# SiLU of a convolution branch: from the Silu table after all tiles to exp, reciprocal and product tile by tile

## The chip, the cores and the metric

The kernel is one program on one core of a Trainium2 chip. The metric is device time in microseconds of the whole program; the time before is the median of three executions. The profile is of one further execution, whose span is counted from its first to its last instruction.

Engines are named as in the profile: PE is TensorE, ACT ScalarE, DVE VectorE, POOL GpSimd, SP the engine that issues nearly all loads. Each takes its instructions strictly in the order in which the program lists them, and semaphores alone tie the engines together.

## The reference, cut to what matters

Two blocks of two layers each run over 512 tokens of 1024 channels in float32. The change lies in the last layer's mixer. It projects the input, runs a forgetting attention with 8 heads of 64 over half of the channels and a convolution branch over the other half, and projects both back:

```
def conformer_conv(p_d, dw_w, dw_b, cn_g, cn_b):
    h = p_d[..., :D_D] * jax.nn.sigmoid(p_d[..., D_D:])
    h = causal_dwconv(h, dw_w) + dw_b              # 31 taps
    h = layer_norm(h, cn_g, cn_b)                  # over 512 channels
    return jax.nn.silu(h)                          # h / (1 + exp(-h))

y_c = forgetting_attention(q, k, v, log_f)
y_d = conformer_conv(p[..., 3 * D_C + H_C:], dw_w, dw_b, cn_g, cn_b)
return jnp.concatenate([y_c, y_d], axis=-1) @ w_out
```

## The kernel before

Every matrix product is made of three PE passes over high and low halves of its operands, so each weight tile that SP loads into `raw` is first split: ACT copies the rounded high half (`split_w`, L464), POOL subtracts it for the low half (L817). Each such tile is called a unit. PE waits for a unit's low half before its first product with it.

The last mixer interleaves everything by hand in a loop over `s` from 0 to 16, written once for each engine. Here it is called step `s`. `p, qb = divmod(s, 4)` is the pair of heads and the block of 128 queries. In step `s` of `p < 3`

- PE makes the logits of both heads (L1580, banks 4 and 5, n = 128 (qb + 1) columns), then projection products for the next pair (L975 to L977); in between it transposes the probabilities of step `s - 1` (`p_transposes`, L1064, banks 6 and 7). At `qb == 0` it also transposes the values (`v_transposes`, L1080, bank 6), at `qb == 1` it multiplies the probabilities of the previous pair with its values (`attend`, L1086, bank 6). From step 12 on the projection products are those of the mixer's output (`odd_out`, L1025 to L1027).
- DVE adds biases and finds the row maximum (`forget_logits`, L2068 and L2071), inverts the row sums (`inverse_sums`, L1769), and copies each finished projection tile out of its bank (L1641: value, Q, K). At `qb == 0` PE does not begin the new logits until DVE has copied the K tile of the step before (`tile_free`).
- ACT takes the exponentials (`exp_row`, L556), scales them (`scale_row`, L565), and copies the transposed probabilities of step `s - 1` out of banks 6 and 7 (`keep_p`, L572).

A bank is written again only once its reader has signalled: 4 and 5 by `lg_free`, 6 and 7 by `tr_free` or `va_free`.

The convolution branch rides along. In steps 5 to 7 its four channel tiles are transposed to tokens through bank 3 (`rows_of`), DVE takes mean and variance of each token, in step 8 ACT scales and shifts the token rows `fz` (L785). In steps 9 and 10 PE transposes them back, one channel tile of 128 x 512 at a time, into bank 3 (`cols_of`, L1533), and ACT copies each into `fC` (`keep_cols`, L724). In step 11, behind its `keep_p`, ACT applies Silu with the channel's gain and bias to all four (L792). Silu stands in another activation table than the exponential, so the profile has an ACT_TABLE_LOAD ahead of the four and another behind them, before the exponentials of step 12 (L556). In steps 12 and 13 ACT and POOL split `fC` into `XH` and `XL` (L476, L831).

ACT splits one unit in each of the steps 1, 5, 9, 12 and 14.

Of the kernel before, what the change touches and what calls it, by code (L numbers as in the profile page):

```python
# [26 lines left out]
F32 = mybir.dt.float32  # L27
F32R = mybir.dt.float32r
ALU = mybir.AluOpType
ACT = mybir.ActivationFunctionType  # L30

P = 128
S = 512
# [132 lines left out]
def build(nc, x, xT, par, con, rcon, gb, w, out):  # L166
    ctx = ExitStack()
    with ctx:
        def sb(name, shape, dt=F32, stack=ctx):
            return stack.enter_context(nc.sbuf_tensor(name, shape, dt))  # L170
# [146 lines left out]
        cwH = sb("cwH", [P, TAPS], F32R, ph)  # L317
        cwL = sb("cwL", [P, TAPS], F32, ph)
        partmax = sb("partmax", [P, 4], F32, ph)
        fBD1 = sb("fBD1", [P, S], F32, ph)  # L320
        fsig = sqt
        fB = [sq, fB1]
# [64 lines left out]
        cn_ready = sem("cn_ready")  # L387
        rows_scaled = sem("rows_scaled")
        to_cols = sem("to_cols")
        cols_kept = sem("cols_kept")  # L390
        swished = sem("swished")
        rows_out = sem("rows_out")
        gate_in = [sem(f"gate_in{i}") for i in range(2)]
        gate_ready = sem("gate_ready")
# [58 lines left out]
        def _(act):  # L453
# [264 lines left out]
                act.wait_ge(to_rows, t + 1)  # L718
                act.copy(fz[t][:, 0:S], bank[3][:]).then_inc(rows_kept, 1)

            def keep_cols(c):

                act.wait_ge(to_cols, c + 1)
                act.copy(fC[:, c, :], bank[3][:]).then_inc(cols_kept, 1)  # L724

            def gate_biases(p):

# [29 lines left out]
            for s in range(17):  # L757
                p, qb = divmod(s, 4)
                if s < 16:
                    n, c = (qb + 1) * P, 2 * (s % 2)  # L760
                    for m in range(2):
                        exp_row(fL[s % 2][m][:, 0:n], negmax[:, c + m:c + m + 1], rowsum[:, c + m:c + m + 1])
                    if qb == 0 and p < 3:
                        gate_biases(p + 1)
                    sums_inverted()
                    for m in range(2):
                        scale_row(fL[s % 2][m][:, 0:n], rinv[:, c + m:c + m + 1])
                    if qb == 0:
                        vax.add()
                if qb == 1 and p:  # L770
                    odd_high(p - 1)
                if s in (6, 7):
                    keep_rows((1, 3)[s - 6])
                if s in (9, 10):
                    keep_cols((0, 2)[s - 9])
                for m in range(2) if s else ():
                    keep_p(fPT[m], 6 + m, (s - 1) % 4)
                if s == 5:
                    keep_conv(3, conv_done, 3)
                if s in (5, 6):  # L780
                    keep_rows((0, 2)[s - 5])
                if s == 8:
                    act.wait_ge(cn_ready, 1)
                    for t in range(NB):
                        act.activation(fz[t][:, 0:S], fz[t][:, 0:S], ACT.Identity, bias=st[:, 3 * NB + t:3 * NB + t + 1],  # L785
                                       scale=root[:, t:t + 1]).then_inc(rows_scaled, 1)
                if s in (9, 10):
                    keep_cols((1, 3)[s - 9])
                if s == 11:
                    act.wait_ge(cols_kept, 4)  # L790
                    for c in range(4):
                        act.activation(fC[:, c, :], fC[:, c, :], ACT.Silu, bias=pcol("cn_b", c), scale=pcol("cn_g", c)).then_inc(swished, 1)  # L792
                if qb == 1 and p < 3 or s in (12, 14):
                    split_w()
                if s == 12:
                    act.wait_ge(tile_free, tiles.at())
                if s in (12, 13):
                    for k in ((4, 5), (6, 7))[s - 12]:
                        split_at(XH[:, k, :], fC[:, k - 4, :], swished, k - 3)
                if p < 3 and qb == 3:  # L800
                    tiles.add(3)
# [7 lines left out]
        def _(pool):  # L809
# [119 lines left out]
            split_w()  # L929
            inverse_root()  # L930
            diagonal_biases(3)
            split_w(2)
            for k in (4, 5, 6, 7):
                split_x(XL[:, k, :], fC[:, k - 4, :], XH[:, k, :])
            split_w()
# [7 lines left out]
        def _(pe):  # L943
# [584 lines left out]
            def cols_of(c):  # L1528

                pe.wait_ge(rows_scaled, NB)  # L1530
                claim(3)
                for t in range(NB):
                    ins = pe.transpose(bank[3][:, t * P:(t + 1) * P], fz[t][:, c * P:(c + 1) * P], ident)  # L1533
                ins.then_inc(to_cols, 1)
                freed[3] = (cols_kept, c + 1)

            def odd_attend(p):

# [31 lines left out]
            for s in range(16):  # L1570
                p, qb = divmod(s, 4)
                i, n = p % 2, (qb + 1) * P
                if qb == 0:
                    pe.wait_ge(tile_free, tiles.at())
                    off = begin_unit()
                claim(4)
                claim(5)
                for m in range(2):
                    half = slice(64 * m, 64 * m + 64)
                    logit_end(pe.matmul(bank[4 + m][:, 0:n], fQ[i][half, qb * P:n], fK[i][half, 0:n], start=True, stop=True), 4 + m)  # L1580
                if qb == 0:
                    v_transposes(6, fVT, tiles.at())
                if qb == 1 and p:
                    odd_attend(p - 1)
                if p < 3:
                    pair_steps(off, ODD_SLOTS[2 * qb])
                    if qb == 3:
                        pair_steps(off, ODD_SLOTS[7])
                elif qb:
                    odd_out((1, 5, 7)[qb - 1])  # L1590
                if s in (6, 7):
                    rows_of((1, 3)[s - 6])
                if s in (9, 10):
                    cols_of((0, 2)[s - 9])
                for m in range(2) if s else ():
                    p_transposes(6 + m, fL[(s - 1) % 2][m], (s - 1) % 4 + 1)
                if p < 3 and qb < 3:
                    pair_steps(off, ODD_SLOTS[2 * qb + 1])
                if s == 14:
                    off = begin_unit()  # L1600
                if p == 3 and qb < 3:
                    odd_out((0, 4, 6)[qb])
                if s in (5, 6):
                    rows_of((0, 2)[s - 5])
                if s in (9, 10):
                    cols_of((1, 3)[s - 9])
            los.add(4)
            for m in range(2):
                p_transposes(6 + m, fL[1][m], NB)
# [7 lines left out]
        def _(dve):  # L1617
# [416 lines left out]
                        ins.then_inc(conv_done, 1)  # L2034

            glu(0)
            dve.wait_ge(cw_hi, 1)
            dve.tensor_tensor(cwL[:], parm[:, PCOL["dw_w"]:PCOL["dw_w"] + 4 * TAPS:4], cwH[:].bitcast(F32), ALU.subtract).then_inc(cw_lo, 1)
            take(lambda: dve.tensor_scalar(lfz[:], bank[2][0:8, :], parm[0:8, PCOL["f_b"]:PCOL["f_b"] + 1], None, ALU.add))
# [44 lines left out]
            for s in range(17):  # L2084
# [24 lines left out]
                if s == 8:  # L2109
                    row_stats(3)  # L2110
                    dve.tensor_scalar(st[:, 2 * NB:3 * NB], moment[:, :, 1], LN_EPS, None, ALU.add).then_inc(var_ready, 1)
                    roots.add()
                    dve.wait_ge(root_ready, roots.at())
                    dve.scalar_tensor_tensor(st[:, 3 * NB:4 * NB], moment[:, :, 0], -1.0, root[:], ALU.mult, ALU.mult).then_inc(cn_ready, 1)
            assert not taps_left
            los.add(5)
            out_projection()
# [121 lines left out]
```

## Time and profile before

| | |
|---|---|
| median of 3 executions | 2341.62 us (2339.07 to 2342.72) |
| the profiled execution, own time | 2339.27 us |
| its span | 2337.5 us |
| PE busy | 2282.1 us, 98% |
| POOL, ACT, DVE busy | 1037.9, 706.2, 703.8 us |
| granted TensorE clock, mean | 0.994 of full |
| chain that ended last: PE | 88% |
| chain that ended last: DVE, ACT | 7%, 3% |
| ACT_TABLE_LOAD, all | 12, 1283 ns each |

The profiled execution's own time is 1.8 us longer than its span: that much lies around it. The two loads that the change speaks of are two of the twelve. A busy share says little for one stage; the stage in question lies between 1870 and 1915 us of the span.

### The profile page before, as it was taken

To read this page: it belongs to the slowest core of one execution; us is meant where nothing else is said; L and a number is where in the kernel's file an instruction comes from. 1 tells how busy PE (TensorE), PEld (TensorE's weight loads), DVE (VectorE), ACT (ScalarE), POOL (GpSimd) and SP (SyncE) were. 2 spreads that over 40 slices of the span, in tenths; PEclk is the share of its full clock that TensorE was granted. 3 is DMA by queue.
4 is the path that set the end of the run, shared out by engine and by line. 5 is a ranking of instruction groups with operands and counts; after the bars stand their busy time and mean duration, and the time that the engine had idled before them with its cause. 6 is when DMAs were issued, how large, how long until landed. Compare 5 with 4: busy or idle time off the path is not lost.

```text
span 2337.5 us, 24617 instructions
## 1 busy us (share of the span) xinstructions
PE 2282.1 (98%) x10287; PEld 1835.8 (79%) x10287; DVE 703.8 (30%) x1351; ACT 706.2 (30%) x1002; POOL 1037.9 (44%) x359
## 2 busy tenths in 40 slices
PE   8999999999999999999999999999999999999998
PEld 6667888888776778888878888888877667888887
DVE  7535000004476450000057320000158635000003
ACT  2443231222344332212222232222244563221220
POOL 3224454454323255545545645445442334554543
PEclk9999999999999999999999999999999999999999
DMA  4213222322221133222223332322222113332221
GB/s 170 72 74 125 104 96 93 106 72 72 90 73 73 54 108 99 99 91 98 99 73 112 108 109 93 106 90 88 79 90 87 51 67 106 111 108 91 93 88 54
DMA packets 33534, 214.72 MB, mean 92 GB/s; under 512 B 3720, under 2 KB 4872, under 8 KB 10000
## 3 DMA queue, kind: packets, MB, share of 16 engines
q1 hardware_dynamic: 32256, 211.03, 26.0%
q10 hardware_dynamic: 1168, 2.11, 0.3%
q8 instruction: 82, 1.34, 0.2%
q14 instruction: 28, 0.23, 0.0%
HBM read 211.02 MB, written 2.11 MB: 91 GB/s over the span
## 4 chain that ended last, share of the span: by engine, by line
PE 88%; DVE 7%; ACT 3%; issue 1%; POOL 0%; DMA 0%; SPq 0%; DVEq 0%; ACTq 0%
PE bank L975 16%; PE bank L977 16%; PE bank L976 16%; PE bank L1025 9%; PE bank L1027 9%; PE bank L1026 9%; DVE bank L2030 2%; PE bank L1086 2%; PE bank L1161 2%; PE bank L1162 2%; PE bank L1166 2%; PE bank L1204 1%; PE bank L1459 1%; PE bank L1006 1%; PE bank L1064 1%
## 5 line engine op out<-in xcount | busy, mean ns | idle before, releaser
L817 POOL TENSOR_TENSOR wlo<-raw,whi 128x2048 fp32r<-128x2048 f32 (+5 forms) x184 | 843.6, 4586 | 603.1 <-ACT whi L464 594.8
L975 PE MATMUL bank<-XH,whi 128*128 128x512 f32 x1752 | 692.1, 395 | 10.8 <-POOL wlo L873 6.1
L977 PE MATMUL bank<-XH,wlo 128*128 128x512 f32 x1752 | 684.6, 391 | 0.0
L976 PE MATMUL bank<-XL,whi 128*128 128x512 f32 x1752 | 683.8, 390 | 0.0
L464 ACT CAST whi<-raw 128x2048 fp32r<-128x2048 f32 (+5 forms) x184 | 349.6, 1901 | 416.5 <-PE bank L1025 304.5
L975 PEld LDWEIGHTS bank<-XH,whi 128*128 128x128 f32 x1752 | 330.4, 189 | 93.5 <-issue 16.3
L977 PEld LDWEIGHTS bank<-XH,wlo 128*128 128x128 f32 x1752 | 330.0, 188 | 69.8
L976 PEld LDWEIGHTS bank<-XL,whi 128*128 128x128 f32 x1752 | 330.5, 189 | 66.5
L1729 DVE TENSOR_TENSOR hf<-sil,bank 128x512 f32<-128x512 f32 x80 | 55.0, 687 | 814.4 <-PE bank L977 814.4
L1025 PE MATMUL bank<-whi,HH 128*128 128x512 f32 x704 | 274.4, 390 | 0.0
L1027 PE MATMUL bank<-wlo,HH 128*128 128x512 f32 x704 | 274.0, 389 | 0.0
L1026 PE MATMUL bank<-whi,HL 128*128 128x512 f32 x704 | 273.9, 389 | 0.0
L831 POOL TENSOR_TENSOR HL<-hf,HH 128x512 fp32r<-128x512 f32 x80 | 103.5, 1294 | 376.2 <-ACT HH L512 376.2
L512 ACT CAST HH<-hf 128x512 fp32r<-128x512 f32 x80 | 49.6, 621 | 453.0 <-DVE hf L1729 453.0
L1025 PEld LDWEIGHTS bank<-whi,HH 128*128 128x128 f32 x704 | 132.1, 188 | 27.4
L1026 PEld LDWEIGHTS bank<-whi,HL 128*128 128x128 f32 x704 | 132.2, 188 | 27.3
L1027 PEld LDWEIGHTS bank<-wlo,HH 128*128 128x128 f32 x704 | 132.1, 188 | 27.4
L1669 DVE SCALAR_TENSOR_TENSOR X<-X,bank 128x512 f32<-128x512 f32 x64 | 43.9, 687 | 278.1 <-PE bank L1027 277.6
L508 ACT ACTIVATE sil<-bank 128x512 f32<-128x512 f32 x80 | 47.8, 598 | 186.2 <-PE bank L977 186.2
L847 POOL TENSOR_TENSOR troot<-tvar,neg_half 128x1 f32<-128x1 f32 x32 | 25.6, 799 | 129.6 <-DVE tvar L1695 129.6
L489 ACT CAST XH<-bank 128x512 fp32r<-128x512 f32 x56 | 30.7, 589 | 155.4 <-PE bank L1204 155.0
L2030 DVE SCALAR_TENSOR_TENSOR bank<-fz,parm,bank 128x512 f32<-128x512 f32 x90 | 68.0, 755 | 3.0
(270 smaller groups left out, 2231.6 us busy)
## 6 DMA issues: line engine op xcount, KB each, us to landing
raw<-w_ffn_gu SPq DMA_DIRECT2D x88, 1024.0 KB, 4.8
raw<-w_ffn_dn SPq DMA_DIRECT2D x40, 1024.0 KB, 4.8
GB<-gb SPq DMA_DIRECT2D x8, 1024.0 KB, 6.8
raw<-w_diff_in SPq DMA_DIRECT2D x6, 1280.0 KB, 6.2
raw<-w_ev_in SPq DMA_DIRECT2D x6, 1024.0 KB, 4.9
raw<-w_od_in SPq DMA_DIRECT2D x4, 1536.0 KB, 6.4
raw<-w_mla_pair SPq DMA_DIRECT2D x4, 1088.0 KB, 5.6
raw<-w_mla_o SPq DMA_DIRECT2D x4, 1024.0 KB, 6.1
```

The lines of the kernel that those rows point to most:

```text
L464: act.copy(whi[:, off:off + size], raw[:, off:off + size]).then_inc(hi_ready, 1)
L512: act.copy(HH[:, j, :], hf[i][:]).then_inc(act_hi, 1)
L817: pool.tensor_tensor(wlo[:, off:off + size], raw[:, off:off + size], whi[:, off:off + size].bitcast(F32), ALU.subtract).then_inc(lo_ready, 1)
L831: pool.tensor_tensor(dst, src, hi.bitcast(F32), ALU.subtract).then_inc(act_lo, 1)
L975: release(pe.matmul(out, whi[:, off:off + P], xh, start=start, stop=False))
L976: pe.matmul(out, whi[:, off:off + P], xl, start=False, stop=False)
L977: return pe.matmul(out, wlo[:, off:off + P], xh, start=False, stop=stop)
L1025: release(pe.matmul(bank[b][:], xh[:, rows], whi[:, off:off + HALF], start=start, stop=False))
L1026: pe.matmul(bank[b][:], xl[:, rows], whi[:, off:off + HALF], start=False, stop=False)
L1027: ins = pe.matmul(bank[b][:], xh[:, rows], wlo[:, off:off + HALF], start=False, stop=stop)
L1729: take(lambda: dve.tensor_tensor(hf[i][:], sil[i][:], bank[2 * i + 1][:], ALU.mult), 2)
L2030: ins = dve.scalar_tensor_tensor(acc, fz[i][:, k:k + S], wk, acc, ALU.mult, ALU.add)
```

## The change: SiLU from the exponential table

`y / (1 + exp(-y))` is worked out with `y = g z + b`, where `z` is the normalised channel tile in bank 3 and `g`, `b` are the channel's gain and bias.

- Once, early in the mixer, DVE makes `negcn`, the negated gains and biases.
- For each channel tile ACT takes `ey = exp(-g z - b)` straight from bank 3. There is one buffer `ey`, so the next exponential waits until the tile before has been finished (`swished`).
- DVE makes `fC = g z + b` from bank 3 (which frees the bank, `norm_kept`), then `ey + 1`, then the reciprocal of it (`inverted`).
- POOL multiplies `fC` by `ey` (`swished`).
- The four tiles are handled in three steps: tile 0 in step 9, 1 and 2 in step 10, 3 in step 11. PE's transposes move with them.
- ACT's weight split of step 9 stands at the end of step 8.

```
-            def keep_cols(c):
+            def exp_cols(c):
                 act.wait_ge(to_cols, c + 1)
-                act.copy(fC[:, c, :], bank[3][:]).then_inc(cols_kept, 1)
+                if c:
+                    act.wait_ge(swished, c)
+                act.activation(ey[:], bank[3][:], ACT.Exp, bias=negcn[:, 4 + c:5 + c], scale=negcn[:, c:c + 1]).then_inc(exp_kept, 1)
...
-                if s in (9, 10):
-                    keep_cols((0, 2)[s - 9])
+                if s in (9, 10, 11):
+                    exp_cols((0, 1, 3)[s - 9])
                 for m in range(2) if s else ():
                     keep_p(fPT[m], 6 + m, (s - 1) % 4)
...
-                if s in (9, 10):
-                    keep_cols((1, 3)[s - 9])
-                if s == 11:
-                    act.wait_ge(cols_kept, 4)
-                    for c in range(4):
-                        act.activation(fC[:, c, :], fC[:, c, :], ACT.Silu, bias=pcol("cn_b", c), scale=pcol("cn_g", c)).then_inc(swished, 1)
-                if qb == 1 and p < 3 or s in (12, 14):
+                if s == 10:
+                    exp_cols(2)
+                if s in (1, 5, 8, 12, 14):
                     split_w()
...
-            split_w(2)
+            def swish(c):
+                pool.wait_ge(inverted, c + 1)
+                pool.tensor_tensor(fC[:, c, :], fC[:, c, :], ey[:], ALU.mult).then_inc(swished, 1)
+            split_w()
+            for c in range(4):
+                swish(c)
+            split_w()
...
-                freed[3] = (cols_kept, c + 1)
+                freed[3] = (norm_kept, c + 1)
...
-                if s in (9, 10):
-                    cols_of((0, 2)[s - 9])
+                if s in (9, 10, 11):
+                    cols_of((0, 1, 3)[s - 9])
...
-                if s in (9, 10):
-                    cols_of((1, 3)[s - 9])
+                if s == 10:
+                    cols_of(2)
...
+            dve.tensor_scalar(negcn[:], parm[:, PCOL["cn_g"]:PCOL["cn_g"] + 8], -1.0, None, ALU.mult)
...
+                for c in {9: (0,), 10: (1, 2), 11: (3,)}.get(s, ()):
+                    dve.wait_ge(exp_kept, c + 1)
+                    dve.tensor_scalar(fC[:, c, :], bank[3][:], pcol("cn_g", c), pcol("cn_b", c), ALU.mult, ALU.add).then_inc(norm_kept, 1)
+                    link(dve.tensor_scalar(ey[:], ey[:], 1.0, None, ALU.add))
+                    dve.reciprocal(ey[:], ey[:]).then_inc(inverted, 1)
```

ACT before, from the copy of the last channel tile (end of step 10) to the first table load behind the four Silu (`fL10`, `fL11` are the logits of step 11, `rinv` its inverted sums):

```order
L724 COPY fC<-bank3 128x512 [waits to_cols]
L556 ACTIVATE fL10,rowsum<-fL10,negmax 128x512 [waits lg_free]
L556 ACTIVATE fL11,rowsum<-fL11,negmax 128x512 [waits lg_free]
L565 ACTIVATE fL10<-fL10,rinv 128x512 [waits rec_ready]
L565 ACTIVATE fL11<-fL11,rinv 128x512
L572 COPY fPT0<-bank6 128x3x128 [waits tr_done]
L572 COPY fPT1<-bank7 128x3x128 [waits tr_done]
L792 ACT_TABLE_LOAD
L792 ACTIVATE fC<-fC,parm 128x512 [waits cols_kept]
L792 ACTIVATE fC<-fC,parm 128x512 x3
L556 ACT_TABLE_LOAD
```

ACT now, the same stretch from the exponential of tile 1 in step 10 to the copies of transposed probabilities in step 11:

```order
L730 ACTIVATE ey<-bank3,negcn 128x512 [waits swished,to_cols]
L576 COPY fPT0<-bank6 128x2x128 [waits tr_done]
L576 COPY fPT1<-bank7 128x2x128 [waits tr_done]
L730 ACTIVATE ey<-bank3,negcn 128x512 [waits swished,to_cols]
L560 ACTIVATE fL10,rowsum<-fL10,negmax 128x512 [waits lg_free]
L560 ACTIVATE fL11,rowsum<-fL11,negmax 128x512 [waits lg_free]
L569 ACTIVATE fL10<-fL10,rinv 128x512 [waits rec_ready]
L569 ACTIVATE fL11<-fL11,rinv 128x512
L730 ACTIVATE ey<-bank3,negcn 128x512 [waits swished,to_cols]
L576 COPY fPT0<-bank6 128x3x128 [waits tr_done]
L576 COPY fPT1<-bank7 128x3x128 [waits tr_done]
```

The two table loads and the four Silu are gone from between the copies and step 12's exponentials; an exponential of a channel tile that waits for `swished` now stands ahead of step 11's row exponentials, and another ahead of its copies.

DVE before, from the inverted row sums of step 10 through the logits of step 11 (ISA is the combined add and minimum of `forget_logits`):

```order
L1769 RECIPROCAL rinv<-rowsum 128x2 [waits exp_done]
L1641 COPY fQ1<-bank1 128x512 [waits tile_done]
L2068 ISA fL10,partmax<-bank4,sq0 128x384 [waits lg_done]
L2068 ISA partmax 128x1
L2071 ISA fL10,negmax<-bank4,shift,partmax 128x128 [waits step]
L2071 ISA negmax 128x1
L2068 ISA fL11,partmax<-bank5,sq1 128x384 [waits lg_done]
L2068 ISA partmax 128x1
L2071 ISA fL11,negmax<-bank5,fBD0,partmax 128x128 [waits step]
L2071 ISA negmax 128x1
L1769 RECIPROCAL rinv<-rowsum 128x2 [waits exp_done]
L1641 COPY fK1<-bank2 128x512 [waits tile_done]
```

DVE now, the same stretch up to the first logits of step 11:

```order
L1780 RECIPROCAL rinv<-rowsum 128x2 [waits exp_done]
L1652 COPY fQ1<-bank1 128x512 [waits tile_done]
L2129 TENSOR_SCALAR fC<-bank3,parm 128x512 [waits exp_kept]
L2130 TENSOR_SCALAR ey<-ey 128x512
L2131 RECIPROCAL ey<-ey 128x512 [waits step]
L2129 TENSOR_SCALAR fC<-bank3,parm 128x512 [waits exp_kept]
L2130 TENSOR_SCALAR ey<-ey 128x512
L2131 RECIPROCAL ey<-ey 128x512 [waits step]
L2080 ISA fL10,partmax<-bank4,sq0 128x384 [waits lg_done]
L2080 ISA partmax 128x1
L2083 ISA fL10,negmax<-bank4,shift,partmax 128x128 [waits step]
L2083 ISA negmax 128x1
```

Six instructions for tiles 1 and 2 have come between the Q tile's copy and the logits of step 11, and the first of each three waits for ACT's exponential.

## Rows read from the trace of the kernel before

**Rows 1.** Page, part 1: busy us, share of span and instructions by engine.
```profile
PE 2282.1 (98%) x10287; PEld 1835.8 (79%) x10287; DVE 703.8 (30%) x1351; ACT 706.2 (30%) x1002; POOL 1037.9 (44%) x359
```

**Rows 2.** ACT in order of time: start us, duration us, engine, line, operation.
```profile
1896.30 1.34 ACT L565 ACTIVATE fL<-fL,rinv 128x512 f32<-128x512 f32 x2 [0.23 <-DVE rinv L1769]
1898.05 0.86 ACT L572 COPY fPT<-bank 128x384 f32<-128x384 f32 x2 [0.41 <-PE bank L1064]
1898.93 1.28 ACT L792 ACT_TABLE_LOAD   x1
1900.22 2.94 ACT L792 ACTIVATE fC<-fC,parm 128x512 f32<-128x512 f32 x4
1903.18 1.28 ACT L556 ACT_TABLE_LOAD   x1
1906.18 1.05 ACT L572 COPY fPT<-bank 128x512 f32<-128x512 f32 x2
```

**Rows 3.** PE in order of time, idle time ahead of it in brackets.
```profile
1876.44 3.93 PE L1086 MATMUL bank<-fPT,fV 128*64 128x512 f32 x16
1883.16 0.60 PE L1533 MATMUL bank<-cons,fz 128*128 128x128 f32 x4
...
1900.42 1.06 PE L1064 MATMUL bank<-cons,fL 128*128 128x128 f32 x8 [0.88 <-DVE fV L2092]
1907.28 5.60 PE L1086 MATMUL bank<-fPT,fV 128*64 128x512 f32 x16 [2.41 <-ACT fPT L572]
```

**Rows 4.** One stretch: busy us by engine, TensorE clock, DMA share, GB/s.
```profile
1907.30:1911.20 3.90, 3.90 (x10) 1.59 (x11) 0.11 (x1) 3.76 (x7) 2.09 (x1) 0.58 0.00 0
```

**Rows 5.** DVE in order of time, steps 10 to 12.
```profile
1886.67 0.42 DVE L2068 CUSTOM_DVE_ANT_0 fL<-bank,sq 128x256 f32<-128x256 f32 x1 [3.98 <-PE bank L1580]
1893.39 0.56 DVE L2068 CUSTOM_DVE_ANT_0 fL<-bank,sq 128x384 f32<-128x384 f32 x1 [3.07 <-PE bank L1580]
1897.72 0.69 DVE L1641 COPY fK<-bank 128x512 f32<-128x512 f32 x1 [1.45 <-PE bank L977]
1899.10 0.29 DVE L2071 CUSTOM_DVE_ANT_0 fL<-bank,sqt 128x128 f32<-128x128 f32 x1 [0.69 <-PE bank L1580]
1899.58 0.69 DVE L2092 COPY fV<-bank 128x512 f32<-128x512 f32 x1
```

**Rows 6.** ACT in order of time, steps 8 to 10.
```profile
1875.07 2.93 ACT L785 ACTIVATE fz<-fz,st,root 128x512 f32<-128x512 f32 x4
1886.32 1.91 ACT L464 CAST whi<-raw 128x2048 fp32r<-128x2048 f32 x1
1889.66 1.12 ACT L565 ACTIVATE fL<-fL,rinv 128x384 f32<-128x384 f32 x2 [0.23 <-DVE rinv L1769]
```

**Rows 7.** By source line: count, ns min/median/max, first and last start.
```profile
L2003 DVE TENSOR_SCALAR EY<-bank,parm x4: 742/744/751, 1282.8 to 1284.8; 128x512 f32<-128x512 f32 x4
L1998 DVE TENSOR_SCALAR EY<-ez,parm x4: 486/722/1007, 1251.5 to 1280.7; 128x512 f32<-128x512 f32 x4
L785 ACT ACTIVATE fz<-fz,st,root x4: 806/808/827, 1875.1 to 1877.2; 128x512 f32<-128x512 f32 x4
L831 POOL TENSOR_TENSOR XL<-fC,XH x4: 1276/1296/1305, 1913.6 to 1918.3; 128x512 fp32r<-128x512 f32 x4
```

**Rows 8.** DVE by source line: two reciprocals, two tensor products.
```profile
L1769 DVE RECIPROCAL rinv<-rowsum x32: 154/166/167, 68.7 to 1929.6; 128x2 f32<-128x2 f32 x32
L1911 DVE RECIPROCAL rinv<-rowsum x32: 162/164/167, 613.7 to 799.1; 128x1 f32<-128x1 f32 x32
L1990 DVE TENSOR_TENSOR EP<-EP,eu x4: 176/176/178, 1227.7 to 1249.9; 128x16 f32<-128x16 f32 x4
L2005 DVE TENSOR_TENSOR EY<-bank,EY x4: 692/692/692, 1289.4 to 1305.8; 128x512 f32<-128x512 f32 x4
```

**Rows 9.** A DVE source line; a POOL weight subtraction in order of time.
```profile
L1985 DVE TENSOR_TENSOR eu<-eu x10: 691/1178/4336, 1226.0 to 1247.3; 128x512 f32<-128x512 f32 x10
1888.31 4.60 POOL L817 TENSOR_TENSOR wlo<-raw,whi 128x2048 fp32r<-128x2048 f32 x1 [9.55 <-ACT whi L464]
```

More of the change, by code:

```diff
@@ L319, in build @@
         partmax = sb("partmax", [P, 4], F32, ph)
+        negcn = sb("negcn", [P, 8], F32, ph)
+        ey = sb("ey", [P, S], F32, ph)
         fBD1 = sb("fBD1", [P, S], F32, ph)
@@ L389, in build @@
         to_cols = sem("to_cols")
-        cols_kept = sem("cols_kept")
         swished = sem("swished")
+        exp_kept = sem("exp_kept")
+        inverted = sem("inverted")
+        norm_kept = sem("norm_kept")
         rows_out = sem("rows_out")
```

## The prediction

> **What bounds the kernel now.** First the page: TensorE is busy for 2282.1 of 2337.5 us and every other engine for less than half [rows 1]. So a change to ACT, DVE or POOL is worth only what PE waits for it, and I read the stage around the change in order of time. PE and ACT first, from the end of step 11. ACT scales the probabilities of step 11 at 1896.30, copies the transposed ones of step 10 until 1898.91, then has the first table load, four Silu and the second load, 1.28 + 2.94 + 1.28 = 5.5 us in which it can serve nobody; its copy of step 11's transposed probabilities ends at 1907.23 [rows 2]. The product of probabilities and values in step 13 needs that copy and sits idle for 2.41 us, until 1907.28 [rows 3]. It then takes 5.60 us where its twin in step 9 took 3.93: the granted clock is 0.58 of full over that stretch [rows 3, 4], a mixture of the two levels, 1.2 and 2.4 GHz, and what came before was PE's idle time. So the Silu block is on the path with 2.41 us of wait and, by the difference of the twins, 1.67 us of slow clock. Earlier PE waits 0.88 us for DVE's copy of the values, which ends at 1900.27 [rows 3, 5]. These 4.96 us are all that this stage can give.
>
> **What goes.** The two loads and four Silu, and four copies out of bank 3. With them the 2.41 us would go, if nothing else were late.
>
> **What comes, per channel tile.** ACT's exponential with two operands per partition: 0.81 us (L785, the same form). DVE: the affine from PSUM 0.74 (L2003); `ey + 1` in SBUF 0.49 (L1998's minimum, a form that reached 1.01 beside POOL) [rows 7]. The reciprocal of 512 columns is not in the trace. Two ends: 0.49 if it went as the fastest SBUF form. For the other end, two columns cost 166 ns and one 164 by the medians, so 2 ns for one more, and 510 of those on 166 make 1.19. The tensor products go from 176 ns at 16 columns to 692 at 512, 1.04 ns a column [rows 8]; at that slope the reciprocal is 0.166 + 0.53 = 0.70, the value I take, since it lies on a row's slope between the ends. DVE per tile: 0.74 + 0.49 + 0.70 = 1.93. POOL's product: 1.30, as L831 [rows 7]. One tile from ACT's start to POOL's end is 0.81 + 1.93 + 1.30 = 4.04 us, and with one buffer `ey` the next may not begin earlier.
>
> **Tile 0, step 9: hidden, with nothing to spare.** ACT's scaling of `fz` ends at 1878.0, the split moved behind it takes 1.91 and ends at 1879.9 [rows 6]. That delays step 9's exponentials by about 1.9 us, but PE is in the product of step 9 until 1880.4 and ACT reaches the cast behind it by 1882.0. The transposes of tile 0 leave PE at 1883.76 [rows 3], exponential until 1884.6, DVE until 1886.5. DVE's logits of step 10 start at 1886.67 before [rows 5] and some 0.4 earlier now, since a group of transposes has gone from ahead of them: late by about nothing. ACT no longer has the 1.91 us split in front of step 10's exponentials, so they are slightly earlier.
>
> **Tiles 1 and 2, step 10: on the path.** DVE's logits of step 10 at 1886.6 lead to ACT's scaling about 2.5 us later, at 1889.1 (step 11 with 512 columns takes 2.91, below), and the scaling takes 1.12 [rows 6]; exponential of tile 1 from 1890.2 to 1891.0; DVE until 1892.95; POOL until 1894.25. ACT stands in front of tile 2's exponential, which ends at 1895.1, and DVE is through at 1897.1. Only then, in DVE's order, come step 11's logits, which were begun at 1893.39: 3.7 us late. Queued behind ACT's wait are step 11's row exponentials, behind DVE's the logits, the inverted sums and the K tile. From the first logit to the scaling it was 1896.30 - 1893.39 = 2.91 [rows 2, 5], so the scaling starts at 1900.0 and the K copy, behind the inverted sums, ends at 1900.7 instead of 1898.41 [rows 5]. PE may not begin step 12 before it: 2.3 us late.
>
> **Tile 3, step 11.** ACT scales until 1901.35, takes tile 3 until 1902.15, copies step 10's transposed probabilities (0.86) until 1903.0 [rows 2]; PE's transposes of values wait for that in bank 6. DVE finishes tile 3 at 1904.1, takes 0.48 for step 12's logits (1899.10 to 1899.58) and 0.69 for the values [rows 5]: 1905.3. PE's transposes of step 11 follow at 1905.35 instead of 1900.42, 4.9 us late.
>
> **Where it ends.** From those transposes to the product in step 13 it was 1907.28 - 1900.42 = 6.86 us, of which 2.41 were the wait [rows 3]. ACT, free of the block, is done with its copy at about 1907.5, so only the 4.45 us of PE work count: the product begins at 1909.8 instead of 1907.28, **2.5 us later**. Three waits (K copy, ACT's bank 6, value copy) of about 2 us each have taken the place of two. They leave PE mostly idle between 1898.5 and 1905.3, more than before, so I expect the slow clock again, a little earlier and at about the same 1.67 us; that term cancels. If it did not come the sum would be +0.8, if it came twice +4.2.
>
> The rest costs nothing that I can see: the first constant `negcn` is one DVE instruction of 0.2 us early in the mixer, ahead of a correction that ACT needs only several small operations later; the high half of the first output unit is ready earlier, its low half by 1884.5,, so the load that waits for its place is issued earlier. Behind step 13 the program is the same and everything moves along.
>
> Sum: the profiled execution's own 2339.27 + 2.5 = 2341.8. The median of the runs lies 2.35 above that execution, so 2344.1 on the scale of the median.
>
> **The unknown costs.** The reciprocal counts three times on the path (tiles 1, 2, 3), and above 0.70 four times, since tile 0 had nothing to spare. At 0.49: 3 x 0.21 = 0.6 less, +1.9. At 1.19: 4 x 0.49 = 2.0 more, +4.5.
>
> **Rival 1, slower: the reciprocal is iterated for every column.** Place: DVE, all four tiles. At eight passes of a row's 1.04 ns per column [rows 8] it is 512 x 8 x 1.04 + 0.16 = 4.42 us, 3.72 more than in my sum, four times over: 14.9, so +17.4 and 2359. It decides from about 1.25 us on, where the sum reaches 0.2%. Against it: a second column would then add 8 ns, and adds 2, and no reciprocal of the 64 took over 167 ns. For it: two columns are few, and a start-up that hides the first passes could look like this. 15%. The Trainium skill speaks for it ("VectorE: DVE Perf Modes", Walkthrough: the 8-slice pipeline in each mode, First, the fixed hardware budget): it says that reciprocal runs by iterative divide with a repeat count of 8 on the same pipe. Whether that count is per column it does not say, and the trace's 2 ns disagree with that reading.
>
> **Rival 2, faster: the waits vanish.** If DVE were through with tile 2 before PE's logits of step 11 (1893.39) [rows 5], nothing would be late, and the 2.41 + 0.88 + 1.67 of today would go: 2336.7. It needs 3.7 us less than two serial tiles cost by the rows; only hand-offs and instructions at half their rows would do. 6%.
>
> **Rival 3, slower: DVE held by POOL.** `ey + 1` is of the form that took 0.49 to 1.01, and a DVE line with two SBUF inputs went from 0.69 to 4.34 us beside POOL [rows 7, 9]. If POOL's subtraction for the unit (4.60 us) [rows 9] began a us later than the 1879.9 worked out, it would still run when tile 0 needs the port at 1885.3, and hold it by up to 4.6 us: +2.5 to +7.1, 2348.7 at most. For: only 0.9 us separate them. Against: nothing that ACT waits for ahead of that split is late. 9%. The Trainium skill has the rule ("SBUF — State Buffer", two separate sides): a Vector operation in a two-port mode and a GpSimd operation lock each other out for a whole instruction. The stretched rows agree.
>
> That the change doesn't do what it says, with table loads elsewhere, I give 1%: between the exponentials of steps 0 and 16 no other table is asked for, and the copies and affines needed none before.
>
> **How the numbers follow.** My case 69%: 2344.1, its own range 2341 to 2347 from the bounds of reciprocal and clock. About 0.2% (4.7 us) is what a measurement of this kernel can tell from no change. Rivals 1 (15%) and 3 (9%, two thirds of it beyond) and 5% of mine above it make slower 0.27; rival 2 makes faster 0.06; the rest is same, 0.67. The range from 2339.5 to 2350 holds mine and rival 3 and leaves out rival 1 and most of 2.
>
> **What would show it.** Two ACT_TABLE_LOAD fewer (10). No ACT idle time ended by PE but two waits of ACT for POOL's product of about 2.5 us ahead of the exponentials of tiles 2 and 3 or of DVE behind them. PE idle three times between 1898 and 1906, put down to DVE's K copy, ACT's copy out of bank 6 and DVE's value copy. No wait of the product in step 13 for ACT. The reciprocal at 0.70 us: above 1.2 my sum fails, at over 4 rival 1 stands. A tile 2 exponential before 1892 would refute the serial chain.

## The result: 2355.1 us, 0.58% slower

After: 2355.11 us, median of 4 runs (2353.68 to 2356.17). Before, on the same chip: 2340.53 us (2339.07 to 2342.72, 4 runs). The ratio is 1.0058, 95% interval 1.0046 to 1.0070, or +13.6 us; the two medians of four lie 14.6 apart. Here and below, us behind a ratio are the ratio times 2340.5. The forecast was 2344.1 with a range up to 2350; it stood on the median of three, 2341.62, which the fourth run has moved to 2340.53. The result lies outside the range, 3.9 us from rival 1's 2359.

The profiled execution took 2354.59 us (span 2352.8). The first reading is the tile `ey`: count, then ns min/median/max, first and last start.

```profile
L730 ACT ACTIVATE ey<-bank,negcn x4: 758/768/781, 1886.9 to 1911.8; 128x512 f32<-128x512 f32 x4
L2130 DVE TENSOR_SCALAR ey<-ey x4: 416/418/419, 1888.5 to 1913.4; 128x512 f32<-128x512 f32 x4
L2131 DVE RECIPROCAL ey<-ey x4: 3352/3353/3354, 1888.9 to 1913.8; 128x512 f32<-128x512 f32 x4
L938 POOL TENSOR_TENSOR fC<-fC,ey x4: 1265/1276/1293, 1892.4 to 1917.2; 128x512 f32<-128x512 f32 x4
```

Three of these four prices are close to those that the sum had from other rows (0.81, 0.49 and 1.30), and the affine that goes with them takes 0.81 instead of 0.74 (below). The reciprocal takes 3.35 us, where the sum had 0.70. Next, what PE waited for in this stretch (1840 to 1975 us), per program line: us in total, times, longest.

```profile
PE bank L1591 <- DVE fK L1652: 6.1, 2, 5.1
PE bank L1075 <- DVE fV L2104: 4.1, 1, 4.1
PE bank L1544 <- DVE fC L2129: 2.9, 1, 2.9
PE bank L1091 <- ACT fPT L576: 2.0, 2, 1.3
```

The kernel before has in the same view 2.4 us for ACT's `fPT` at the product and 0.9 for DVE's values [rows 3]. DVE in order of time shows why (start, duration, engine, line, operation, idle time ahead):

```profile
1888.92 3.35 DVE L2131 RECIPROCAL ey<-ey 128x512 f32<-128x512 f32 x1
1892.19 0.36 DVE L2080 CUSTOM_DVE_ANT_0 fL<-bank,sq 128x256 f32<-128x256 f32 x1
...
1896.49 0.81 DVE L2129 TENSOR_SCALAR fC<-bank,parm 128x512 f32<-128x512 f32 x1 [1.27 <-ACT ey L730]
1897.21 0.42 DVE L2130 TENSOR_SCALAR ey<-ey 128x512 f32<-128x512 f32 x1
1897.67 3.35 DVE L2131 RECIPROCAL ey<-ey 128x512 f32<-128x512 f32 x1
1903.30 0.81 DVE L2129 TENSOR_SCALAR fC<-bank,parm 128x512 f32<-128x512 f32 x1 [2.28 <-ACT ey L730]
1904.03 0.42 DVE L2130 TENSOR_SCALAR ey<-ey 128x512 f32<-128x512 f32 x1
1904.48 3.35 DVE L2131 RECIPROCAL ey<-ey 128x512 f32<-128x512 f32 x1
1907.75 0.49 DVE L2080 CUSTOM_DVE_ANT_0 fL<-bank,sq 128x384 f32<-128x384 f32 x1
...
1910.48 0.67 DVE L1652 COPY fK<-bank 128x512 f32<-128x512 f32 x1
...
1913.81 3.35 DVE L2131 RECIPROCAL ey<-ey 128x512 f32<-128x512 f32 x1
...
1917.45 0.69 DVE L2104 COPY fV<-bank 128x512 f32<-128x512 f32 x1
```

These answer to [rows 5]. The row maxima of step 11 (L2080) stand behind the tiles 1 and 2 and start at 1907.75 instead of 1893.39; the K copy starts at 1910.48 instead of 1897.72, the value copy at 1917.45 instead of 1899.58. ACT waits in between for POOL, and then for those maxima:

```profile
1902.49 0.78 ACT L730 ACTIVATE ey<-bank,negcn 128x512 f32<-128x512 f32 x1 [5.50 <-POOL fC L938]
1908.68 0.72 ACT L560 ACTIVATE fL<-fL,negmax 128x512 f32<-128x512 f32 x1 [5.41 <-DVE negmax L2083]
```

PE sits idle ahead of four of these (answering to [rows 3]):

```profile
1897.45 0.79 PE L1544 MATMUL bank<-cons,fz 128*128 128x128 f32 x4 [2.91 <-DVE fC L2129]
1898.16 2.08 PE L1591 MATMUL bank<-fK,fQ 64*128 64x512 f32 x4
...
1911.21 0.63 PE L1591 MATMUL bank<-fK,fQ 64*128 64x128 f32 x4 [5.11 <-DVE fK L1652]
1913.11 1.09 PE L1091 MATMUL bank<-cons,fVT 128*128 128x128 f32 x4 [1.27 <-ACT fPT L576]
1918.28 1.94 PE L1075 MATMUL bank<-cons,fL 128*128 128x128 f32 x8 [4.08 <-DVE fV L2104]
...
1924.26 3.93 PE L1097 MATMUL bank<-fPT,fV 128*64 128x512 f32 x16
```

The product of step 13 waits for nothing and runs at its fast 3.93 us. The clock was low earlier instead, each time behind idle time of PE (columns as in [rows 4]):

```profile
1895.00:1900.00 5.00, 2.55 (x8) 0.93 (x8) 3.70 (x4) 1.99 (x5) 0.00 (x0) 0.78 0.00 0
...
1910.00:1915.00 5.00, 1.72 (x8) 1.05 (x8) 3.08 (x5) 3.12 (x7) 0.00 (x0) 0.64 0.00 2
1915.00:1920.00 5.00, 1.72 (x9) 1.75 (x9) 3.30 (x7) 2.16 (x7) 1.27 (x1) 0.50 0.00 0
1920.00:1925.00 5.00, 5.00 (x20) 3.29 (x19) 0.61 (x5) 3.42 (x4) 2.27 (x1) 0.83 0.00 0
```

I set the start of each PE instruction against its twin before. When the stage begins the two executions are already 3.1 us apart, gained and lost in steps at about 743, 804, 1214 and 1720 us in code that the change does not touch (the last section has the cause). At the logits of step 11 the difference is 5.9, at the K copy's reader 12.7, at step 11's transposes 17.9, at step 13's product 17.0, and behind it 15.3. So the stage itself cost 12.2 us; times below with "own" are such differences, each of one pair of executions, with the earlier shift taken off.

### The profile page after: what moved, and what is told of

Same layout as the page of the kernel before. It is cut to its first block, busy times and chain, and to the rows that moved or that the text cites. A ratio compares the mean times of both kernels' runs of the same rounds, so it can differ in the third digit from the quotient of the medians.

```text
span 2352.8 us, 24630 instructions
## 1 busy us (share of the span) xinstructions
PE 2288.5 (97%) x10287; PEld 1841.7 (78%) x10287; DVE 720.9 (31%) x1364; ACT 701.4 (30%) x996; POOL 1042.7 (44%) x363
## 4 chain that ended last, share of the span: by engine, by line
PE 87%; DVE 8%; ACT 3%; issue 1%; POOL 0%; DMA 0%; SPq 0%; DVEq 0%; ACTq 0%
PE bank L986 16%; PE bank L987 16%; PE bank L988 16%; PE bank L1036 9%; PE bank L1038 9%; PE bank L1037 9%; DVE bank L2041 2%; PE bank L1097 2%; PE bank L1172 2%; PE bank L1173 2%; PE bank L1177 2%; PE bank L1215 1%; PE bank L1017 1%; PE bank L1470 1%; PE bank L1075 1%
```

## The experiments

The theory: the mechanism of the forecast is right and one price in it is wrong, the reciprocal at 512 columns, which counts four times. The rivals: the chain over three engines costs more than its instructions, or the time on VectorE costs by its amount wherever it stands. All ratios are to the kernel before on the same chip.

**Without the reciprocal** (a cheap operation in its place; the result is not SiLU).

```
-                    dve.reciprocal(ey[:], ey[:]).then_inc(inverted, 1)
+                    dve.tensor_scalar(ey[:], ey[:], 1.0, None, ALU.min).then_inc(inverted, 1)
```

> The changed kernel with its four reciprocals of 128x512 (3.35 us each in its trace) replaced by a minimum with 1.0 in place, one cheap instruction; the convolution branch's values are no longer the reference's. My theory: the reciprocal's size alone turned +2.5 us into +13.6. Then this kernel falls back to +1 us against the kernel before (range -1 to +4: 0.7 by the working of the prediction with 0.42 in place of 0.70, and one stretch of slow clock more or less), with DVE's instruction at about 0.42 us. Rival: the serial chain over one buffer and the hand-offs cost it, whatever the reciprocal takes. Then most of the 13.6 stays, +8 or more.

Measured: 2341.4 us (2340.99 to 2344.03), ratio 1.0007 (0.9998 to 1.0016), +1.6 us. The operation took 0.43 us, PE's waits shrank to these:

```profile
PE bank L1091 <- ACT fPT L576: 2.1, 2, 1.4
...
PE bank L1075 <- DVE fV L2104: 1.3, 1, 1.3
...
PE bank L1591 <- DVE fK L1652: 0.8, 1, 0.8
```

The prediction's lower bound, a reciprocal at 0.49, gave +1.9. Chain, hand-offs, moved split and the two table loads come out in total as the sum had them; own it is +1.3. The single waits do not: the forecast had three of about 2 us.

**Half of the columns** (the other 256 are not inverted).

```
-                    dve.reciprocal(ey[:], ey[:]).then_inc(inverted, 1)
+                    dve.reciprocal(ey[:, 0:256], ey[:, 0:256]).then_inc(inverted, 1)
```

> The changed kernel with each reciprocal over 256 of the 512 columns only (the other half of the branch is left wrong). Theory: the reciprocal costs 6.24 ns a column, so it takes 1.75 us, and as it stands in the way three to four times the kernel is 5 to 8 us over the kernel before, about halfway. Rival (a threshold: once DVE is late at all, the same waits come): it stays within 2 us of the changed kernel, +11.5 or more.

Measured: 2349.66 us (2345.73 to 2350.04), ratio 1.0033 (1.0021 to 1.0046), +7.7 us.

```profile
L2131 DVE RECIPROCAL ey<-ey x4: 1752/1753/1754, 1890.4 to 1910.5; 128x256 f32<-128x256 f32 x4
```

0.43, 1.75 and 3.35 us of this operation give +1.6, +7.7 and +13.6 us. The intervals are too wide for slopes (this one alone is 4.9 to 10.8 us). Own it is +1.3, +5.9 and +12.2: 3.4 us of time per us of the operation in the first step, 4.0 in the second, about the four that the forecast counted.

**The price by itself.** The kernel before, with reciprocals of 1 to 512 columns in the first feed-forward part.

```
+    n = ((1, 2, 3, 4, 8, 16, 32, 64, 128, 256, 384, 512) if half == 0
+         else (512, 256, 128, 64, 32, 16, 8, 4, 2, 1))[j]
+    link(dve.reciprocal(sqt[:, 0:n], sqt[:, 0:n]))
+    link(dve.tensor_scalar(sqt[:, 0:n], sqt[:, 0:n], 1.0, None, ALU.add))
```

> The kernel before, with reciprocals of 1, 2, 3, 4, 8, 16, 32, 64, 128, 256, 384 and 512 columns of 128 partitions put on VectorE in the first feed-forward part (twice, up and down), each followed by a sum of the same columns. It measures the disputed price by itself. The profile of the changed kernel had 3.353 us at 512 columns, the half reciprocal 1.753 us at 256; a straight line through both is 0.153 us and 6.25 ns a column. Theory (the iterated reciprocal takes its time column by column from the first one on): 3 columns 0.17, 16 columns 0.25, 64 columns 0.55, 128 columns 0.95, 384 columns 2.55 us, and one against two columns differ by 6 ns, within a clock tick or so of what the kernel before showed (2 ns). Rival (the slope begins only with wide rows, so narrow ones could never have told): 16 columns 0.16 to 0.18 us and 64 columns under 0.3 us. The sums stay near 1 ns a column: 0.6 us or less at 512.

Measured (count, then after the bar busy us and mean ns of one); the kernel took 2341.69 us in its one run, the kernel before 2341.68 in the median:

```profile
L1736 DVE RECIPROCAL sqt<-sqt 128x512 f32<-128x512 f32 x2 | 6.7, 3346 | 0.0
L1736 DVE RECIPROCAL sqt<-sqt 128x256 f32<-128x256 f32 x2 | 3.5, 1747 | 0.0
...
L1736 DVE RECIPROCAL sqt<-sqt 128x64 f32<-128x64 f32 x2 | 1.1, 546 | 0.0
...
L1736 DVE RECIPROCAL sqt<-sqt 128x16 f32<-128x16 f32 x2 | 0.5, 246 | 0.0
L1736 DVE RECIPROCAL sqt<-sqt 128x8 f32<-128x8 f32 x2 | 0.4, 196 | 0.0
...
L1736 DVE RECIPROCAL sqt<-sqt 128x4 f32<-128x4 f32 x2 | 0.3, 170 | 0.0
...
L1736 DVE RECIPROCAL sqt<-sqt 128x2 f32<-128x2 f32 x1 | 0.2, 157 | 0.0
L1736 DVE RECIPROCAL sqt<-sqt 128x1 f32<-128x1 f32 x1 | 0.2, 156 | 0.0
```

From 8 columns up it is (3346 - 196) / 504 = 6.25 ns a column and 0.146 us besides, to a few ns at every width. Below that the steps are uneven: 1 ns from 1 to 2 columns, the step that I had read, and 13 ns from 2 to 4. The rival (a slope that starts with wide rows) falls: a 16-column reciprocal would have told it. The expectation for the sums, 0.6 us or less at 512 columns, failed: they took 4.13, and the last section says why.

**The four reciprocals without the chain.** The kernel before, SiLU on ACT and all, with four reciprocals on a scratch buffer at the change's places in DVE's queue.

```
+                for c in {9: (0,), 10: (1, 2), 11: (3,)}.get(s, ()):
+                    link(dve.reciprocal(ey[:], ey[:]))
```

> The kernel before with its four SiLUs and copies as they were, and four reciprocals of 512 columns on a scratch buffer at the places in VectorE's queue where the change has its own (step 9 one, step 10 two, step 11 one): the time on VectorE, 4 x 3.35 = 13.4 us, without the chain to ScalarE and GpSimd. Theory (a reciprocal costs what the chain makes of it: the K copy of step 10, the values of step 11 stand behind it, but the waits for the exponentials add more): VectorE has 5 to 7 us of idle time a step in steps 9 to 11, so only part of each reciprocal stands in front of what TensorE waits for: +2 to +6 us, 2342.5 to 2346. Rival (the time on VectorE is all of it, the chain nothing): as the changed kernel, +12 to +14 us. The other rival (VectorE's idle time hides it): within 1 us of before.

Measured: 2344.04 us (2340.29 to 2346.18), ratio 1.0011 (1.0001 to 1.0020), +2.6 us. The same 13.4 us of DVE account for 13.6 - 1.6 = 12.0 us in the changed kernel. Part of the difference is that the kernel before still has its 2.41 us wait of the product, in which a delay can hide: at step 11's transposes, ahead of that wait, these four cost 4.6 us own, and in the changed kernel 14.7 less the 3.3 that the form without reciprocals shows there, 11.4. The rest, about 7 us, comes through the chain: each reciprocal waits for ACT's exponential, which waits for the maxima or for POOL, which wait for the reciprocal before. It is seen at the first one. Here it starts at 1882.82, straight behind DVE's copy, is over before the logits of step 10 are ready, and their maxima start 0.1 us late own; in the changed kernel it has to wait for the exponential until 1888.92, and the same maxima are 2.4 us late own. At step 11's maxima it is 3.6 against 11.2. The rival (time on VectorE is all of it) falls.

```profile
1882.82 3.34 DVE L2118 RECIPROCAL ey<-ey 128x512 f32<-128x512 f32 x1
1887.00 0.42 DVE L2070 CUSTOM_DVE_ANT_0 fL<-bank,sq 128x256 f32<-128x256 f32 x1 [0.83 <-PE bank L1581]
```

**Two buffers in the changed kernel**, which takes ACT's wait for POOL away.

```
-                if c:
-                    act.wait_ge(swished, c)
+                if c > 1:
+                    act.wait_ge(swished, c - 1)
```

with `eys[c % 2]` for `ey` on all engines.

> The changed kernel with a second buffer for the exponential (1 of 2, by turns; it is the idle half of a table of constants), so that ScalarE no longer waits for GpSimd's product of the tile before: its idle 5.50 us in front of tile 2's exponential goes. All reciprocals are there. Theory (what stands in front of TensorE's waits are VectorE's reciprocals, and ScalarE's wait is one link of it): the chain of the tiles is shortened by at most 2 to 3 us, +9 to +12 us over the kernel before, 2350 to 2352.5. Rival (the one buffer, with its turn round three engines, is what costs): at most +5 us, 2345.

Measured: 2352.5 us (2350.92 to 2355.72), ratio 1.0049 (1.0036 to 1.0062), +11.5 us. The K copy's wait fell from 6.1 to 4.3 us, the others stayed. The intervals of the two kernels overlap; own the stage costs 11.3 instead of 12.2. So the one buffer was worth 1 to 2 us and is not what made the kernel slow. Part of what it freed was lost at once: tile 2's sum now starts at 1903.61, while POOL multiplies tile 1 (1903.15 to 1904.45), and takes 1.11 us instead of 0.42.

**Two buffers and later places.** Tile 2's sum and reciprocal move behind step 11's maxima and K copy, tile 3's behind step 12's value copy, tile 3's exponential behind ACT's copies of the probabilities.

```
-                for c in {9: (0,), 10: (1, 2), 11: (3,)}.get(s, ()):
+                for c in {9: (0,), 10: (1, 2), 12: (3,)}.get(s, ()):
                     dve.wait_ge(exp_kept, c + 1)
                     ... the affine out of bank 3
+                for c in {9: (0,), 10: (1,), 11: (2,), 12: (3,)}.get(s, ()):
                     ... the sum and the reciprocal
```

> The changed kernel with two buffers for the exponential, and with the places of the tanh form that was faster: all four reciprocals of 3.35 us are still there and GpSimd still multiplies, but tile 2's sum and reciprocal stand behind step 11's row maxima on VectorE, tile 3's behind step 12's row maxima and value copy, and tile 3's exponential behind ScalarE's copies of the probabilities. Theory (a long operation costs by what is queued behind it: in the changed kernel two reciprocals stood one behind the other in front of step 11's row maxima, and the third in front of the value copy): TensorE's waits for the K copy and the values, 5.1 and 4.1 us in the changed kernel, fall under 2 us each; at most a reciprocal of tile 2 in front of step 12's maxima stays. +1 to +6 us against the kernel before, 2343 to 2348. Rival (the 13.4 us of VectorE's time cost by their amount, wherever they stand): +9 to +12 us, as with two buffers alone.

Measured: 2346.92 us (2344.49 to 2349.66), ratio 1.0019 (1.0010 to 1.0028), +4.4 us, where the same work in the places of the change cost +11.5 (own 5.5 and 11.3).

```profile
PE bank L1076 <- DVE fV L2105: 2.9, 1, 2.9
PE bank L1545 <- DVE fC L2130: 2.9, 1, 2.9
PE bank L1592 <- DVE fK L1653: 1.7, 2, 1.0
```

The K copy's wait is down to 1.7, as expected. The values' 2.9 is over the 2 us I had asked for: tile 2's reciprocal (1908.86 to 1912.21) now stands in front of step 12's maxima and of the value copy. The 2.9 of L1545 is tile 0's reciprocal, in front of step 10's maxima and of tile 1's affine, which frees bank 3; it had not moved.

**How much there was to gain.** The kernel before with Identity for Silu: no table loads (the result is not SiLU).

```
-  act.activation(fC[:, c, :], fC[:, c, :], ACT.Silu, bias=..., scale=...)
+  act.activation(fC[:, c, :], fC[:, c, :], ACT.Identity, bias=..., scale=...)
```

> The kernel before with Identity in place of the four Silu of step 11, same operands and bias and scale: the two table loads go, the four activations stay; the branch has no SiLU. It prices the gain that the change reached for. Theory: the table loads take 2.57 us of ACT on the path, PE's wait of 2.41 us in step 13 goes, -2.5 us, and -4 if the stretch of slow clock behind it goes too. Rival: the wait moves to the next late hand-off (ACT's copy out of bank 6) and the gain is under 1 us.

Measured: 2337.74 us (2335.63 to 2340.81), ratio 0.9989 (0.9980 to 0.9998), -2.6 us; by PE's offsets about the stage -4.1 own, 2.41 of wait and 1.67 of slow clock, as read from [rows 3]. Of this 0.4 us is lost again just behind, where PE waits for POOL's low half of `fC` (L831), so 3.7 reach the end.

**SiLU by tanh, without a reciprocal.** y/2 (1 + tanh(y/2)), tanh on ACT, one DVE operation for sum and product, POOL without part in it, the constants halved instead of negated, two buffers, in the change's places.

```
-                    link(dve.tensor_scalar(ey[:], ey[:], 1.0, None, ALU.add))
-                    dve.reciprocal(ey[:], ey[:]).then_inc(inverted, 1)
+                    dve.wait_ge(norm_kept, c + 1)
+                    dve.scalar_tensor_tensor(fC[:, c, :], eys[c % 2], 1.0, fC[:, c, :], ALU.add, ALU.mult)
```

> A version without reciprocal: silu(y) = (y/2)(1 + tanh(y/2)), tanh from the table that is already loaded. ACT takes tanh of a channel tile from bank 3 into one of two buffers, DVE makes y/2 from bank 3 (0.81 us) and (tanh + 1) times it in SBUF (0.75 us), POOL has no part; places in the steps as in the changed kernel. Theory (what a tile holds DVE and ACT for decides): DVE per tile 1.56 instead of 4.6 us, no wait for POOL, so about -1 us against the kernel before, -3 if the slow clock of step 13 goes. Rival: the placement itself, work of the branch ahead of step 11's and 12's logits, costs: +2 us or more.

Measured: 2339.71 us (2338.25 to 2343.23), ratio 0.9996 (0.9987 to 1.0005), -0.9 us with zero in the interval, own -1.1. PE still waited 1.6 us for the values (tile 3's 1.5 us of DVE stand ahead of their copy) and 0.8 for ACT.

**The same in later places** (the loops of the exponential's late form, with the one product instead of sum and reciprocal).

> SiLU as (y/2) (1 + tanh(y/2)), as in the run before of that form (two VectorE operations of 0.81 and 0.69 us a tile, no reciprocal, GpSimd without it), with the places changed: tile 3's tanh behind ScalarE's copies of the transposed probabilities in step 11, tile 2's product behind step 11's row maxima, tile 3's sum and product behind step 12's row maxima and value copy. Theory (in the first placing tile 3's 1.50 us stood in front of the value copy, PE waiting 1.60 us, and the tanh of 0.76 us in front of the copy of the probabilities, PE waiting 0.83 us, with a stretch of slow clock after): both waits fall under 0.5 us, step 13's product at full clock and about 1.5 to 3 us earlier; -2 to -4 us against the kernel before, 2336 to 2338. Rival (those waits are hidden again further on, or upstream shifts swamp them): as the first placing, within 1 us of before.

Measured: 2338.49 us (2333.62 to 2340.09, 11 runs), ratio 0.9986 (0.9977 to 0.9995), -3.3 us: below the kernel before by more than its interval, though under the 0.2% named in the prediction, and with an interval that overlaps the first placing's. PE in order of time:

```profile
1898.93 1.06 PE L1068 MATMUL bank<-cons,fL 128*128 128x128 f32 x8 [0.88 <-DVE fV L2097]
...
1903.31 3.93 PE L1090 MATMUL bank<-fPT,fV 128*64 128x512 f32 x16
```

The wait for ACT is gone, that for the values back at the 0.88 of before (not under 0.5, as I had expected), and step 13's product runs at the fast 3.93 without a wait: -4.0 us own, nearly all of the 4.1 that the switch of tables can give.

## Why the prediction was wrong

**What bounds the kernel: right.** 2.41 us of wait and 1.67 of slow clock behind the Silu block, 4.1 in all, came back when the tables no longer switched. In every run the own difference was made of PE's waits in this stage and of the slow clock behind them.

**The step that failed** is the sentence "The tensor products go from 176 ns at 16 columns to 692 at 512, 1.04 ns a column; at that slope the reciprocal is 0.166 + 0.53 = 0.70, the value I take". It measured 3.35 us, and this term counts four times in the sum. The slope belonged to another operation. The upper end, 1.19, was no bound either: it took 2 ns a column from the medians of two lines whose own instructions scatter from 154 to 167 ns [rows 8]. The slowest of two columns and the fastest of one, 167 and 162, already allow 5 ns a column, 2.7 us. With the whole scatter of 13 ns as the error of a reading it is up to 6.8 us, and only there the right 6.25 ns a column lies inside.

**The mechanism, rival 1's, was stated but priced at 15%.** Its objection, that a second column would add 8 ns, had the same fault: in the sweep the second column adds 1 ns, the step from 2 to 4 adds 13, and from 8 on each adds 6.25. Its price of 4.42 us was 32% too high. In terms of DVE's 1.04 ns a column [rows 8] a column takes 6.0 passes; that it is passes of an iteration is the reading, the time per column is what is shown. The Trainium skill's "VectorE: DVE Perf Modes" (Walkthrough: the 8-slice pipeline in each mode) speaks of a repeat count of 8; the sweep does not show eight passes a column.

**The chain: right, with the measured price put in.** The sum had the start of step 13's product 2.5 us late and counted the reciprocal four times: 2.5 + 4 x (3.35 - 0.70) = 13.1; measured 13.9 own at its start and 12.2 behind it. Step 10's maxima: about nothing + 2.65; measured 2.4 own. Step 11's maxima: 3.7 + 3 x 2.65 = 11.7; measured 11.2 own. Step 11's transposes: 4.9 + 10.6 = 15.5; measured 14.7 own. With 3.35 in the same working the forecast would have been +13.1 and 2354.7; measured were +13.6 by the ratio, +12.2 own, and 2355.1. That 2354.7 and 2355.1 lie so close is in part luck: the working misses by up to 0.9 at single points, and the median that it starts from has moved by 1.1.

**The waits: right in name, not in number.** PE idle for the K copy, ACT's bank 6 and the value copy came in that order, and the product's wait for ACT is gone. A fourth, 2.9 us for bank 3, I did not have: at 0.70 it hardly exists (0.2 without the reciprocal). Of two waits of ACT for POOL by about 2.5 us one came, of 5.5; ahead of tile 3 ACT waited for the maxima of step 11 instead.

**The clock: right that it cancels, wrong in place and number.** There were two slow stretches. One, from 1897 to 1901, slowed the logits of step 11 (2.08 us, and 1.13 in the kernel before, in the row below) and what stands around them, by 1.6 us in all; it cost nothing, since PE then waited 5.11 us for the K copy, which hangs on DVE's chain. The other began with step 11's transposes: from there to the product PE takes 5.98 us instead of the 4.45 of the sum. These 1.5 us stand in place of the 1.67 of before.

```profile
1892.23 1.13 PE L1580 MATMUL bank<-fK,fQ 64*128 64x512 f32 x4
```

**Rival 2** (nothing late) needed shorter operations than exist in this form; the tanh form in later places is what comes near it. **Rival 3** (DVE held by POOL) did not happen, with the margin that it was given: POOL's subtraction ended at 1887.60, tile 0's sum began 0.87 us later (0.9 in the text), and all four sums took 0.42. **Table loads**: 12 before, 10 after, as said.

**The range.** Its upper end took the 1.19 for a bound. With 2.7 us in its place the sum is 2352, with 6.8 past 2360.

## What to carry to other kernels

Before a price is taken from another operation's slope, or from two rows of nearly the same width, set the scatter of the rows against the difference: if it is larger, the row gives no slope, and the range has to be as wide as the scatter allows. A long operation in an in-order queue costs by what stands behind it and by whether it is a link in a chain that comes back to the same queue: here the same 13.4 us of reciprocals cost 2.6 us off the chain and about 12 in it, and the kernel with all of them +11.5 or +4.4 by their places alone. When a table switch is the target, look first for a function of the loaded table that needs no division.

## What the hardware showed that I had not expected

**A VectorE sum of one SBUF operand waits out a GpSimd operation that is already running, a reciprocal does not.** In the run of widths each reciprocal was followed by a sum of the same columns. The first two rows are DVE's, the last two POOL's, in order of time:

```profile
346.44 3.35 DVE L1736 RECIPROCAL sqt<-sqt 128x512 f32<-128x512 f32 x1
349.82 4.13 DVE L1737 TENSOR_SCALAR sqt<-sqt 128x512 f32<-128x512 f32 x1
```

```profile
347.25 1.30 POOL L831 TENSOR_TENSOR HL<-hf,HH 128x512 fp32r<-128x512 f32 x1 [4.30 <-ACT HH L512]
349.06 4.61 POOL L817 TENSOR_TENSOR wlo<-raw,whi 128x2048 fp32r<-128x2048 f32 x1 [0.51 <-ACT whi L464]
```

The sum takes 4.13 us, ten times its 0.42, and ends at 353.95, 0.28 after POOL's subtraction; its twin at 425.98 does the same. At 384 columns the sum began 0.04 us before the subtraction and took 0.36. The reciprocal, begun first, neither held POOL's 1.30 us operation nor was held. For the other order there are two rows of the four reciprocals without the chain, where the first of the two began 1.94 us into POOL's subtraction:

```profile
1890.45 6.73 DVE L2118 RECIPROCAL ey<-ey 128x512 f32<-128x512 f32 x2
```

```profile
1888.51 4.59 POOL L818 TENSOR_TENSOR wlo<-raw,whi 128x2048 fp32r<-128x2048 f32 x1 [9.54 <-ACT whi L465]
```

It took its usual 3.34, and the subtraction its usual 4.59. For the sum this is the rule weighed under rival 3 ("SBUF — State Buffer", two separate sides, in the Trainium skill), that a Vector operation in a two-port mode and a GpSimd operation lock each other out for a whole instruction; the trace agrees, with 4.13 us for the sum behind a subtraction of 4.61. In the changed kernel the subtraction (1882.99 to 1887.60) was over 0.87 us before the first sum, and then POOL waited for the reciprocals.

**Equal code drifts by microseconds between executions, mostly by the clock.** In code that the experiments did not touch, PE's starts differ from those of the kernel before by -1.7 to +5.2 us when the stage begins, over the changed kernel and eight of the experiments. Steps come in the first 80 us, whose cause is open, and at a few later places, about 743, 804, 1214 and 1720 us above all. In the changed kernel against the one before, one of the two has the low clock at each of these four, or has it for longer (1720). The kernel before and the changed one at the largest (columns as in [rows 4]):

```profile
1213.00:1219.00 6.00, 5.78 (x29) 4.51 (x28) 2.86 (x9) 4.90 (x4) 2.13 (x1) 1.00 0.00 0
```

```profile
1213.00:1219.00 6.00, 5.98 (x19) 4.77 (x18) 2.90 (x9) 4.66 (x4) 1.51 (x1) 0.54 0.00 0
```

A matmul of 512 columns takes 0.39 us in the first and 0.63 in the second, and 2.3 us are lost. What decides which of the two an execution gets is open. The whole time goes the same way: of 27 executions of the kernel before, the 14 with a mean granted clock of 0.994 or more took 2337.3 to 2340.0 us and the other 13 took 2340.2 to 2344.1. So an effect of 3 us has to be read from offsets about its own stage, or from many runs.
